# Reading the activations and writing the PSUM banks in woven blocks of four, in a two-layer transformer step

## The chip, the cores and the metric

The kernel runs on one core of one Trainium2 chip. The metric is device time in microseconds, the median of 3 runs of the program. In the views TensorE is named PE, its weight loads PEld, VectorE DVE, ScalarE ACT, GpSimd POOL and SyncE SP.

## What is computed

One inference step of a backbone of two layers on 128 context tokens and 128 latent tokens, with D_MODEL 2048 and float32 weights. Cut to its products:

```python
h = rms_norm(x, g_attn) * (1 + scale1) + shift1
proj = h @ w_in                                           # 2048 x 3584
...
x = x + gate1 * (concat(y_conv, y_g, y_w) @ w_out)        # 2048 x 2048
h2 = rms_norm(x, g_mlp) * (1 + scale2) + shift2
x = x + gate2 * (square(relu(h2 @ w_mlp1)) @ w_mlp2)      # 2048 x 8192, 8192 x 2048
```

Between the two lines of products stand the conv module and two groups of attention heads. `shift`, `scale` and `gate` come from a product of a conditioning vector with `w_ada` (2048 x 12288 per layer). Every weight serves both sets of tokens, so the kernel treats them as 256 columns.

## The kernel before, in words

**The split.** Each product with `w_in`, `w_out`, `w_mlp1` and `w_mlp2` is made to nearly float32 accuracy out of float32r operands. A weight W is split in `hi` (W rounded, ScalarE, L889) and `lo` (W - hi, VectorE, L1219), an activation X in the same way. The kernel adds hi x X_hi, hi x X_lo and lo x X_hi. The activations lie in `hs` (input of `w_in` and `w_mlp1`) and `act2` (input of `w_out` and `w_mlp2`), both `[128, 16, 512]`: for each of 16 k-tiles 256 hi values, one per token, and behind them 256 lo values, 1 KiB each.

**The matmuls.** The weights are the stationary operand, the activations the moving one, and the outputs are features x tokens. A PSUM bank holds 512 float32 values. For each k and each of two output tiles j, one matmul of 512 columns multiplies `hi` with X_hi and X_lo at once and writes the whole bank `pb[2g+j]` (L643, and L742 in the mixers' stage), and one of 256 columns multiplies `lo` with X_hi and adds into the bank's columns 256 to 511 (L646, L745). Per k the order is hi j=0, hi j=1, lo j=0, lo j=1. Four k make a chunk, four chunks a half (g), two halves a pair; a pair covers 512 output features. `walk` sets the order of pairs: 7 for `w_in`, 4 for `w_out`, then 4 times (4 up, 4 down), per layer. All engines follow the same walk.

**The evacuation.** After a half, a bank holds hi x X_hi in its first 256 columns and the other two terms in its last 256. ScalarE copies the last 256 to `tmp` (`copies`, L981), VectorE adds the first 256 to it (L1355 into `tsum` in `pair`; L1418 into `zc` or `zq` and L1426 into `tsum` in the mixers) and raises `bank_freed`. PE waits for `bank_freed` before it writes the same bank again, that is after the other half. The halves that close a norm use one 256-column sum instead, with three matmuls per k and j (`one_sum` L682, L685; `last_slices` L668, L670), and need no `tmp`; the first two pairs of `w_in` (`open_chunk`, L568, L571) also use matmuls of 256 columns.

**The rest of the order.** SP loads weights, 1 MB per DMA, each behind a wait on `lo_ready`. The buffers of `hi` and `lo` form a ring of four chunks: ACT waits for `half_used` (PE done with a chunk) to fill `hi`, DVE waits for `hi_ready`, PE waits for `lo_ready`. POOL loads `w_ada` for the units of L532, which PE multiplies at set places between chunks, with 32 weight columns and four matmuls of 512 columns side by side. L700 in `column_sums` multiplies a float32 matrix of ones with float32 tiles of 256 columns, for the conv module's layer norm. L1255 (`gains`) works out `amul` with operands whose innermost run is the two sets of tokens.

Of the kernel before, what the change touches and what calls it, by code (L numbers as in the profile page):

```python
# [6 lines left out]
ALU = mybir.AluOpType  # L24
ACT = mybir.ActivationFunctionType
AX = mybir.AxisListType

P = 128
# [23 lines left out]
ACT2_LAYER = MIX_STEPS + KT * CHUNKS  # L52
RES_LAYER = KT * (1 + CHUNKS)
UNROLL_K = 4

# [56 lines left out]
def build(nc, t):  # L114
# [93 lines left out]
    sinT = cst[:, C_SIN:C_SIN + P]  # L208
    sel = cst[:, C_SEL:C_SEL + 8]
    sel_q = cst[:, C_SELQ:C_SELQ + 4]  # L210

    def sem(name):
        return nc.alloc_semaphore(name)
# [185 lines left out]
    with block:  # L399
# [97 lines left out]
        def _(pe):  # L497
# [121 lines left out]
            for l in range(DEPTH):  # L619
                def pair(kind, n, i, c, a, last, l=l):  # L620
                    acts = act2 if kind in ("out", "down") else hs
                    for g in range(2):
                        fresh = g == 0 and kind == "up" and isinstance(i, int) and i == 0 \
                            and isinstance(c, int) and c == 0

                        after(pe, bank_freed, 4 * n + 2 * g - 2 - sums_left_out(l, kind))
                        for h in range(4):
                            pe.wait_ge(lo_ready, 8 * n + 4 * g + h + 1)
                            if kind == "down":
                                pe.wait_ge(act2_ready, hidden_base(l, c) + 4 * (h + 1))  # L630
                            elif kind == "up" and not fresh:
                                pe.wait_ge(hs_ready, (2 * l + 1) * NORM_STEPS + 8 * (h + 1))
                            if closes_norm(kind, i, g) and h == 3:
                                mm = last_slices(g, acts)
                            for k in range(4 if not (closes_norm(kind, i, g) and h == 3) else 0):
                                if fresh:
                                    pe.wait_ge(hs_ready, (2 * l + 1) * NORM_STEPS + 8 * h + 2 * (k + 1))
                                k_ = 4 * h + k
                                if closes_norm(kind, i, g):
                                    mm = one_sum(g, h, k, acts)  # L640
                                    continue
                                for j in range(2):
                                    pe.matmul(pb[2 * g + j][:, :], hi[:, h, k, j * P:(j + 1) * P], acts[:, k_, :],  # L643
                                              start=(k_ == 0), stop=False)
                                for j in range(2):
                                    mm = pe.matmul(pb[2 * g + j][:, TOK:2 * TOK], lo[:, h, k, j * P:(j + 1) * P],  # L646
                                                   acts[:, k_, 0:TOK], start=False, stop=(k_ == KT - 1))
                            mm.then_inc(half_used, 1)
                            if last and 4 * g + h in (2, 4, 6):
                                turn_tiles(2 * g + h // 2 - 1)  # L650
                            if a is not None and kind == "out" and h == 2:
                                for u in range(2):
                                    ada_unit(*vector_of(kind, i, a, c), a, 4 * quarter(kind, i, a) + 2 * g + u)
                            if a is not None and kind == "up" and g == 1 and h == 2:
                                for u in range(2 if follows_norm(kind, i, c) else 0, 4):
                                    ada_unit(*vector_of(kind, i, a, c), a, 4 * quarter(kind, i, a) + u)
                    if a is not None and quarter(kind, i, a) == 3:
                        vl, vm = vector_of(kind, i, a, c)
                        ada_turn(vl * VECTORS + vm)
# [79 lines left out]

                def slice_products(g, x, k, slot, acts, start, stop):  # L740
                    for j in range(2):
                        pe.matmul(pb[2 * g + j][:, :], hi[:, slot, k, j * P:(j + 1) * P], acts[:, 4 * x + k, :],  # L742
                                  start=start, stop=False)
                    for j in range(2):
                        mm = pe.matmul(pb[2 * g + j][:, TOK:2 * TOK], lo[:, slot, k, j * P:(j + 1) * P],  # L745
                                       acts[:, 4 * x + k, 0:TOK], start=False, stop=stop)
                    return mm

                def unit(l, u):
# [133 lines left out]
        def _(act):  # L883
# [59 lines left out]
            for l in range(DEPTH):  # L943
# [34 lines left out]
                def copies(kind, n, g, l=l):  # L978
                    for j in range(2):
                        after(act, bank_freed, 4 * n + 2 * g + j - 1 - sums_left_out(l, kind))  # L980
                        act.activation(tmp[:, j, :], pb[2 * g + j][:, TOK:2 * TOK], ACT.Copy).then_inc(tmp_ready, 1)  # L981

                def residual_square(c, i, g, j, l=l):
                    r = res_tiles(l, c) + 4 * i + 2 * g + j
# [229 lines left out]
        def _(dve):  # L1214
# [115 lines left out]
            for l in range(DEPTH):  # L1330
                def pair(kind, n, i, c, a, last, l=l):
# [4 lines left out]
                    for g in range(2):  # L1336
# [6 lines left out]
                        for j in range(2):  # L1343
                            tile = bass.ds(4 * i + 2 * g + j, 1)
                            done = 4 * n + 2 * g + j + 1
                            bank = pb[2 * g + j][:, 0:TOK]
                            if closes_norm(kind, i, g):
                                if j == 0:
                                    dve.wait_ge(first_closed, 2 * l + (kind == "down") + 1)
                                else:  # L1350
                                    dve.wait_ge(half_used, 8 * n + 8)
                                residual(kind, i, g, j, bank.rearrange("p (m q) -> p m q", m=1))
                                continue
                            dve.wait_ge(tmp_ready, done - sums_left_out(l, kind))
                            dve.tensor_tensor(tsum[:, j, :], bank, tmp[:, j, :], ALU.add).then_inc(bank_freed, 1)  # L1355
                            dve.wait_ge(bank_freed, done - sums_left_out(l, kind))
                            if kind == "up":
                                dve.scalar_tensor_tensor(thid[:, j, :], tsum[:, j, :], 0.0, tsum[:, j, :],  # L1358
                                                         ALU.max, ALU.mult).then_inc(relu2_ready, 1)
                            else:  # L1360
                                residual(kind, i, g, j, tsum[:, j:j + 1, :])
# [38 lines left out]
                def mixers(l):  # L1400
                    n = l * PAIRS_LAYER
                    for step in range(OPEN_STEPS if l == 0 else 0, 8 * (IN + 1)):
                        p, g = step // 8, step // 4 % 2
                        for e in range(2 * HEADS):
                            if step == score_step(e) + 1:
                                maxima(l, e)
                        if l == 0 or step:
                            split_lo(n + p, step % 8 + 3)
                        mix_ops(l, step)
                        if step % 4 == 3 and p < IN:  # L1410
                            z, first = (zc, CONV_TILES[p][g]) if p < 2 else (zq, ZQ_TILES[p][g])
                            if p == 5 and g == 0:
                                dve.wait_ge(turn_ready, 4 * l + 2)
                            elif p >= 5:
                                dve.wait_ge(score_ready, 2 * HEADS * l + (2 if p == 5 else 4 + 2 * g))
                            for j in range(2):
                                dve.wait_ge(tmp_ready, 4 * (n + p) + 2 * g + j + 1 - sums_left_out(l, "in"))
                                dve.tensor_tensor(z[:, first + j, :], pb[2 * g + j][:, 0:TOK], tmp[:, j, :], ALU.add)\  # L1418
                                   .then_inc(bank_freed, 1)
                    n += IN  # L1420
                    dve.memset(ssq[:, :], 0.0).then_inc(ssq_steps, 1)
                    for g in range(2):
                        for j in range(2):
                            done = 4 * n + 2 * g + j + 1
                            dve.wait_ge(tmp_ready, done - sums_left_out(l, "out"))
                            dve.tensor_tensor(tsum[:, j, :], pb[2 * g + j][:, 0:TOK], tmp[:, j, :], ALU.add)\  # L1426
                               .then_inc(bank_freed, 1)
                            dve.wait_ge(bank_freed, done - sums_left_out(l, "out"))
                            residual("out", 0, g, j, tsum[:, j:j + 1, :])
                        for j in range(2):  # L1430
                            square_sum(-1, 0, g, j)
# [275 lines left out]
```

## Time and profile before

| | |
|---|---|
| median of 3 runs | 2276.07 us (2275.89 to 2277.03) |
| span of the profiled execution | 2273.1 us |
| PE busy | 2221.1 us, 98% |
| DVE, ACT busy | 1448.4 us (64%), 1140.3 us (50%) |
| granted clock, mean | 0.991 of 2.4 GHz |
| HBM read | 565.76 MB; read and written 250 GB/s over the span |

The profile gives the profiled execution's span, from its first to its last instruction, and no other time of its own; the median is 3.0 us above that span. The ends of matmuls are modelled, and matmuls overlap in the pipeline: a group's mean duration is longer than the distance from one start to the next, and durations of a stage add up to more than the stage.

### The profile page before, as it was taken

What the parts mean: (1) busy time and instruction counts of PE and PEld (TensorE: products, weight loads), DVE (VectorE), ACT (ScalarE), POOL (GpSimd) and SP (SyncE); (2) the same over time, 40 slices, a digit from 0 to 9 for tenths busy, and PEclk for the clock granted to TensorE, in tenths of its full rate; (3) what the DMA queues carried; (4) which work ended last, traced back from release to release, by engine and by line L of the source; (5) the groups of instructions that cost most, each with busy time, mean ns of one, the idle gap of its engine ahead of it and who ended that gap; (6) DMA issues with size and microseconds to landing.
All of it is one profiled execution on the core that took longest, in us unless ns stands there. A gap on an engine that the chain in (4) does not pass through costs nothing. (4 is left out here: it accounts for less than half of the span.)

```text
span 2273.1 us, 36235 instructions
## 1 busy us (share of the span) xinstructions
PE 2221.1 (98%) x13534; PEld 1828.8 (80%) x13534; DVE 1448.4 (64%) x2481; ACT 1140.3 (50%) x1890; POOL 95.6 (4%) x185
## 2 busy tenths in 40 slices
PE   6899999999999999999999999999999999999998
PEld 3577777778877887887787777887788888888887
DVE  2377765755655665565567876676566666666665
ACT  2255664644544444454456466665445545445444
POOL 1000100000000000000000000000000000000000
PEclk8899999999999999999999999999999999999999
DMA  9998878887588578758756877667756556656653
GB/s 377 406 365 304 298 275 316 310 319 260 185 306 323 186 246 309 259 185 305 276 186 239 309 290 282 225 203 260 255 187 187 186 185 186 188 184 200 190 186 106
DMA packets 398512, 570.70 MB, mean 251 GB/s; under 512 B 10232, under 2 KB 356464, under 8 KB 377648
## 3 DMA queue, kind: packets, MB, share of 16 engines
q1 hardware_dynamic: 372368, 398.77, 53.4%
q0 software_dynamic: 23712, 168.08, 18.6%
q10 hardware_dynamic: 2304, 2.10, 0.3%
q8 instruction: 86, 1.41, 0.2%
q14 instruction: 42, 0.34, 0.0%
HBM read 565.76 MB, written 3.15 MB: 250 GB/s over the span
## 5 line engine op out<-in xcount | busy, mean ns | idle before, releaser
L1219 DVE TENSOR_TENSOR lo<-raw,hi 128x1024 fp32r<-128x1024 f32 x688 | 824.7, 1223 | 428.1 <-ACT hi L889 427.0
L889 ACT ACTIVATE hi<-raw 128x1024 fp32r<-128x1024 f32 x688 | 709.7, 1054 | 449.4 <-PE bank L646 308.1
L643 PE MATMUL bank<-act,hi 128*128 128x512 f32 x2304 | 724.7, 396 | 1.2 <-DVE tsum L1426 1.2
L643 PE MATMUL bank<-hs,hi 128*128 128x512 f32 x2048 | 647.0, 397 | 0.2
L646 PEld LDWEIGHTS bank<-act,lo 128*128 128x128 f32 x2304 | 432.8, 188 | 102.3
L646 PEld LDWEIGHTS bank<-hs,lo 128*128 128x128 f32 x2048 | 384.7, 188 | 91.0
L646 PE MATMUL bank<-act,lo 128*128 128x256 f32 x2304 | 452.6, 278 | 0.0
L646 PE MATMUL bank<-hs,lo 128*128 128x256 f32 x2048 | 402.4, 278 | 0.0
L643 PEld LDWEIGHTS bank<-act,hi 128*128 128x128 f32 x2304 | 350.7, 189 | 5.6 <-issue 3.4
L643 PEld LDWEIGHTS bank<-hs,hi 128*128 128x128 f32 x2048 | 311.5, 189 | 20.8 <-issue 20.2
L981 ACT ACTIVATE tmp<-bank 128x256 f32<-128x256 f32 x328 | 108.0, 381 | 357.9 <-PE bank L646 294.3
L742 PE MATMUL bank<-hs,hi 128*128 128x512 f32 x768 | 247.4, 403 | 1.5 <-DVE lo L1219 1.5
L1355 DVE TENSOR_TENSOR tsum<-bank,tmp 128x256 f32<-128x256 f32 x272 | 114.5, 421 | 198.5 <-ACT tmp L981 198.5
L745 PEld LDWEIGHTS bank<-hs,lo 128*128 128x128 f32 x768 | 144.2, 188 | 34.1
L745 PE MATMUL bank<-hs,lo 128*128 128x256 f32 x768 | 151.4, 278 | 0.0
L987 ACT ACTIVATE thid<-xT 128x256 f32 (+1 forms) x160 | 66.8, 418 | 157.5 <-DVE xT L1389 153.5
L742 PEld LDWEIGHTS bank<-hs,hi 128*128 128x128 f32 x768 | 117.3, 189 | 14.5 <-issue 9.5
L532 PE MATMUL bank<-ada,cT 128*32 128x512 f32 x960 | 119.3, 609 | 3.5 <-DMA ada<-in_w_ada 2.6
L474 POOL DMA_DIRECT2D ada<-in_w_ada x120 | 63.6, 530 | 1391.3 <-PE bank L532 1285.9
L1389 DVE SCALAR_TENSOR_TENSOR xT<-tsum,mods,xT 128x128 f32 (+1 forms) x304 | 93.5, 349 | 34.9 <-DVE tsum L1355 33.6
L1509 DVE SCALAR_TENSOR_TENSOR yconv<-hpad,vecs,yconv 128x256 f32<-128x256 f32 x240 | 100.5, 479 | 0.0
L965 ACT ACTIVATE act<-thid 128x256 fp32r<-128x256 f32 x128 | 53.5, 418 | 69.7 <-DVE thid L1358 69.7
(179 smaller groups left out, 1360.0 us busy)
## 6 DMA issues: line engine op xcount, KB each, us to landing
raw<-in_w_mlp SPq DMA_DIRECT2D x256, 1024.0 KB, 6.2
ada<-in_w_ada POOLq DMA_DIRECT2D x120, 1024.0 KB, 7.5
raw<-in_w_in SPq DMA_DIRECT2D x56, 1024.0 KB, 5.9
ring_q<-in_w_ada POOLq DMA_DIRECT2D x40, 1024.0 KB, 11.5
raw<-in_w_out SPq DMA_DIRECT2D x32, 1024.0 KB, 5.5
pre_a<-in_w_ada SPq DMA_DIRECT2D x32, 512.0 KB, 10.8
pre_q<-in_w_ada SPq DMA_DIRECT2D x16, 512.0 KB, 10.6
ada<-in_w_ada SPq DMA_DIRECT2D x16, 512.0 KB, 10.6
```

What stands on the lines that cost most here:

```text
L532: mm = pe.matmul(ada_ps[32 * q:32 * q + 32, :], cT[:, k, :], unit[:, q * 512:(q + 1) * 512], start=(k == 0), stop=(k == KT - 1))
L643: pe.matmul(pb[2 * g + j][:, :], hi[:, h, k, j * P:(j + 1) * P], acts[:, k_, :], start=(k_ == 0), stop=False)
L646: mm = pe.matmul(pb[2 * g + j][:, TOK:2 * TOK], lo[:, h, k, j * P:(j + 1) * P], acts[:, k_, 0:TOK], start=False, stop=(k_ == KT - 1))
L742: pe.matmul(pb[2 * g + j][:, :], hi[:, slot, k, j * P:(j + 1) * P], acts[:, 4 * x + k, :], start=start, stop=False)
L745: mm = pe.matmul(pb[2 * g + j][:, TOK:2 * TOK], lo[:, slot, k, j * P:(j + 1) * P], acts[:, 4 * x + k, 0:TOK], start=False, stop=stop)
L889: act.activation(hi[:, o % 4, :, :], raw_chunk(n, o, s, sub), ACT.Copy).then_inc(hi_ready, 1)
L981: act.activation(tmp[:, j, :], pb[2 * g + j][:, TOK:2 * TOK], ACT.Copy).then_inc(tmp_ready, 1)
L987: act.activation(thid[:, j:j + 1, :], xT[:, bass.ds(4 * i + 2 * g + j, 1), :], ACT.Square).then_inc(sq_ready, 1)
L1219: dve.tensor_tensor(lo[:, o % 4, :, :], raw_chunk(n, o, s, sub), hi[:, o % 4, :, :].bitcast(f32), ALU.subtract).then_inc(lo_ready, 1)
L1355: dve.tensor_tensor(tsum[:, j, :], bank, tmp[:, j, :], ALU.add).then_inc(bank_freed, 1)
L1389: dve.scalar_tensor_tensor(x, total[:, :, s * P:(s + 1) * P], mods[:, l, bass.ds(gate + 4 * i + 2 * g + j, 1), s], x, ALU.mult, ALU.add).t ...
L1509: dve.scalar_tensor_tensor(y, hpad[:, ch, :, tap:tap + P], vecs[:, l, 1, 4 * tap + ch:4 * tap + ch + 1], y, ALU.mult, ALU.add).then_inc(co ...
```

## The change

It alters access patterns alone: no instruction, wait, buffer or DMA is added, removed or moved, and the layout of `hs` and `act2` stays. The hi matmul reads its 512 moving values in blocks of four: four of X_hi, the four of X_lo of the same tokens, the next four of X_hi, and so on (`woven`), and writes the bank in one run, which so holds the two kinds in alternating blocks of four. The lo matmul reads X_hi in order and adds into every second block of four (`strand(bank, 1)`). The evacuations read the bank's two strands in blocks of four (L981, L1355, L1418, L1426). `one_sum`, `last_slices` and `open_chunk` are as before.

```diff
WEAVE = 4
...
@@ -209,6 +193,20 @@
     sel = cst[:, C_SEL:C_SEL + 8]
     sel_q = cst[:, C_SELQ:C_SELQ + 4]
 
+    def woven(tiles, k):
+
+
+        return tiles[:, k, :].rearrange("p (t b e) -> p b t e", t=2, e=WEAVE)
+
+    def strand(bank, t):
+
+
+        return bank.rearrange("p (b t e) -> p b t e", t=2, e=WEAVE)[:, :, t, :]
+
+    def blocks(ap):
+
+        return ap.rearrange("p (b e) -> p b e", e=WEAVE)
+
     def sem(name):
         return nc.alloc_semaphore(name)
 
@@ -640,11 +638,11 @@
                                     mm = one_sum(g, h, k, acts)
                                     continue
                                 for j in range(2):
-                                    pe.matmul(pb[2 * g + j][:, :], hi[:, h, k, j * P:(j + 1) * P], acts[:, k_, :],
+                                    pe.matmul(pb[2 * g + j][:, :], hi[:, h, k, j * P:(j + 1) * P], woven(acts, k_),
                                               start=(k_ == 0), stop=False)
                                 for j in range(2):
-                                    mm = pe.matmul(pb[2 * g + j][:, TOK:2 * TOK], lo[:, h, k, j * P:(j + 1) * P],
-                                                   acts[:, k_, 0:TOK], start=False, stop=(k_ == KT - 1))
+                                    mm = pe.matmul(strand(pb[2 * g + j][:, :], 1), lo[:, h, k, j * P:(j + 1) * P],
+                                                   blocks(acts[:, k_, 0:TOK]), start=False, stop=(k_ == KT - 1))
                             mm.then_inc(half_used, 1)
                             if last and 4 * g + h in (2, 4, 6):
                                 turn_tiles(2 * g + h // 2 - 1)
@@ -739,11 +737,11 @@
 
                 def slice_products(g, x, k, slot, acts, start, stop):
                     for j in range(2):
-                        pe.matmul(pb[2 * g + j][:, :], hi[:, slot, k, j * P:(j + 1) * P], acts[:, 4 * x + k, :],
+                        pe.matmul(pb[2 * g + j][:, :], hi[:, slot, k, j * P:(j + 1) * P], woven(acts, 4 * x + k),
                                   start=start, stop=False)
                     for j in range(2):
-                        mm = pe.matmul(pb[2 * g + j][:, TOK:2 * TOK], lo[:, slot, k, j * P:(j + 1) * P],
-                                       acts[:, 4 * x + k, 0:TOK], start=False, stop=stop)
+                        mm = pe.matmul(strand(pb[2 * g + j][:, :], 1), lo[:, slot, k, j * P:(j + 1) * P],
+                                       blocks(acts[:, 4 * x + k, 0:TOK]), start=False, stop=stop)
                     return mm
 
                 def unit(l, u):
@@ -978,7 +976,7 @@
                 def copies(kind, n, g, l=l):
                     for j in range(2):
                         after(act, bank_freed, 4 * n + 2 * g + j - 1 - sums_left_out(l, kind))
-                        act.activation(tmp[:, j, :], pb[2 * g + j][:, TOK:2 * TOK], ACT.Copy).then_inc(tmp_ready, 1)
+                        act.activation(blocks(tmp[:, j, :]), strand(pb[2 * g + j][:, :], 1), ACT.Copy).then_inc(tmp_ready, 1)
 
                 def residual_square(c, i, g, j, l=l):
                     r = res_tiles(l, c) + 4 * i + 2 * g + j
@@ -1352,7 +1350,8 @@
                                 residual(kind, i, g, j, bank.rearrange("p (m q) -> p m q", m=1))
                                 continue
                             dve.wait_ge(tmp_ready, done - sums_left_out(l, kind))
-                            dve.tensor_tensor(tsum[:, j, :], bank, tmp[:, j, :], ALU.add).then_inc(bank_freed, 1)
+                            dve.tensor_tensor(blocks(tsum[:, j, :]), strand(pb[2 * g + j][:, :], 0), blocks(tmp[:, j, :]),
+                                              ALU.add).then_inc(bank_freed, 1)
                             dve.wait_ge(bank_freed, done - sums_left_out(l, kind))
                             if kind == "up":
                                 dve.scalar_tensor_tensor(thid[:, j, :], tsum[:, j, :], 0.0, tsum[:, j, :],
@@ -1415,16 +1414,16 @@
                                 dve.wait_ge(score_ready, 2 * HEADS * l + (2 if p == 5 else 4 + 2 * g))
                             for j in range(2):
                                 dve.wait_ge(tmp_ready, 4 * (n + p) + 2 * g + j + 1 - sums_left_out(l, "in"))
-                                dve.tensor_tensor(z[:, first + j, :], pb[2 * g + j][:, 0:TOK], tmp[:, j, :], ALU.add)\
-                                   .then_inc(bank_freed, 1)
+                                dve.tensor_tensor(blocks(z[:, first + j, :]), strand(pb[2 * g + j][:, :], 0),
+                                                  blocks(tmp[:, j, :]), ALU.add).then_inc(bank_freed, 1)
                     n += IN
                     dve.memset(ssq[:, :], 0.0).then_inc(ssq_steps, 1)
                     for g in range(2):
                         for j in range(2):
                             done = 4 * n + 2 * g + j + 1
                             dve.wait_ge(tmp_ready, done - sums_left_out(l, "out"))
-                            dve.tensor_tensor(tsum[:, j, :], pb[2 * g + j][:, 0:TOK], tmp[:, j, :], ALU.add)\
-                               .then_inc(bank_freed, 1)
+                            dve.tensor_tensor(blocks(tsum[:, j, :]), strand(pb[2 * g + j][:, :], 0),
+                                              blocks(tmp[:, j, :]), ALU.add).then_inc(bank_freed, 1)
                             dve.wait_ge(bank_freed, done - sums_left_out(l, "out"))
                             residual("out", 0, g, j, tsum[:, j:j + 1, :])
                         for j in range(2):
```

## Rows read from the trace of the kernel before

**Rows 1.** The page: span, and busy time by engine (us, share, instructions).

```profile
span 2273.1 us, 36235 instructions
...
PE 2221.1 (98%) x13534; PEld 1828.8 (80%) x13534; DVE 1448.4 (64%) x2481; ACT 1140.3 (50%) x1890; POOL 95.6 (4%) x185
```

**Rows 2.** The page: the span in 40 slices, PE busy and granted clock, in tenths.

```profile
PE   6899999999999999999999999999999999999998
...
PEclk8899999999999999999999999999999999999999
```

**Rows 3.** Waits of PE and its weight loads: us in all, times, longest.

```profile
PEld bank L643 <- issue: 23.5, 32, 1.2
...
PEld bank L742 <- DVE lo L1219: 4.2, 5, 0.8
...
  PEld bank L643: 1.4, 1
```

**Rows 4.** Groups by shape: busy us, mean ns, idle before.

```profile
L643 PE MATMUL bank<-act,hi 128*128 128x512 f32 x2304 | 724.7, 396 | 1.2 <-DVE tsum L1426 1.2
...
L643 PE MATMUL bank<-hs,hi 128*128 128x512 f32 x2048 | 647.0, 397 | 0.2
...
L742 PE MATMUL bank<-hs,hi 128*128 128x512 f32 x768 | 247.4, 403 | 1.5 <-DVE lo L1219 1.5
...
L742 PE MATMUL bank<-act,hi 128*128 128x512 f32 x128 | 41.1, 402 | 0.7 <-DVE act L1491 0.7
```

**Rows 5.** 1950 to 2200 us: PE, PEld, DVE, ACT, POOL busy (x); then L643 alone.

```profile
1950.00:2200.00 250.00, 250.00 (x1438) 218.12 (x1437) 164.43 (x247) 124.80 (x180) 0.00 (x0) 1.00 0.59 185
...
1950.00:2200.00 250.00, 225.45 (x718) 109.20 (x719) 1.00 0.59 185
```

**Rows 6.** Chain from 1800 to 1812 us: start, us, what.

```profile
1800.34 0.47 PE bank L643 x2
1800.81 0.23 PE bank L646 x2
1801.04 0.46 PE bank L643 x2
```

**Rows 7.** PE at half clock, 39 to 45 us: start, us, instructions.

```profile
39.00:45.00 6.00, 3.75 (x17) 3.75 (x18) 5.60 (x9) 3.74 (x4) 0.00 (x0) 0.50 1.05 407
...
42.70 1.05 PE L568 MATMUL bank<-hs,hi 128*128 128x256 f32 x4
43.56 0.63 PE L571 MATMUL bank<-hs,lo 128*128 128x256 f32 x2
```

**Rows 8.** PE at 1200 us, L668 and L670 by turns, 256 columns each.

```profile
1199.94 0.40 PE L668 MATMUL bank<-act,hi 128*128 128x256 f32 x2
...
1200.66 0.40 PE L668 MATMUL bank<-act,hi 128*128 128x256 f32 x2
```

**Rows 9.** PE at 1407 us: L700; then its durations, min/median/max ns.

```profile
1407.32 1.02 PE L700 MATMUL bank<-ysq,ones 128*128 128x256 f32 x4
...
L700 PE MATMUL bank<-ysq,ones x16: 377/378/381, 266.9 to 1408.0; 128*128 128x256 f32 x16
```

**Rows 10.** Chain, longest pieces: start, us, what.

```profile
1233.32 1.85 PE bank L532 x16
```

**Rows 11.** Groups by shape on DVE and ACT: busy us, mean ns.

```profile
L1219 DVE TENSOR_TENSOR lo<-raw,hi 128x1024 fp32r<-128x1024 f32 x688 | 824.7, 1223 | 428.1 <-ACT hi L889 427.0
...
L889 ACT ACTIVATE hi<-raw 128x1024 fp32r<-128x1024 f32 x688 | 709.7, 1054 | 449.4 <-PE bank L646 308.1 <-PE bank L745 83.0 <-DMA raw<-in_w_in 49.6
...
L1355 DVE TENSOR_TENSOR tsum<-bank,tmp 128x256 f32<-128x256 f32 x272 | 114.5, 421 | 198.5 <-ACT tmp L981 198.5
...
L981 ACT ACTIVATE tmp<-bank 128x256 f32<-128x256 f32 x328 | 108.0, 381 | 357.9 <-PE bank L646 294.3 <-PE bank L745 63.6
...
L1255 DVE SCALAR_TENSOR_TENSOR amul<-mods,vecs 128x8 f32<-128x8 f32 x4 | 0.7, 168 | 0.1
...
L1255 DVE SCALAR_TENSOR_TENSOR amul<-mods,vecs 128x32 f32<-128x32 f32 x3 | 0.6, 185 | 0.0
```

More of the change, by code:

```diff
@@ L54 @@
 UNROLL_K = 4
+WEAVE = 4
 IN_COLS = ((0, 512), (256, 768), (1792, 1024), (1280, 1536), (2048, 3072), (2304, 2560), (2816, 3328))
```

## The prediction, made before the change was run

> **What bounds the kernel now.** First the shares: PE is busy for 2221.1 us of a span of 2273.1, 98%; DVE has 64% and ACT 50% [rows 1], and from the fifth slice on PE is full in every slice at full granted clock (2.4 GHz) [rows 2]. Then the waits of PE: a wait for a filled lo buffer costs L742 4.2 us in all, and L643 stands 23.5 us at "issue" [rows 3]. So the end is set by how fast TensorE takes matmuls from its own stream. Then the groups by shape: 5248 matmuls with the 512-column hi weights' product (2304 + 2048 at L643, 768 + 128 at L742), and as many lo products of 256 columns, since the code issues two of each per k [rows 4].
>
> A duration of 396 ns is not what one costs, since they overlap. The last full stage has 1438 matmuls in 250 us, 718 of them hi [rows 5]: per k (two hi, two lo) 4 x 250/1438 = 0.695 us. The chain splits that: two hi take 0.46 or 0.47 us, two lo 0.23 (17 pairs of each kind stand in these 12 us, all in this beat) [rows 6]. So **a hi costs about 0.233 us and a lo 0.115**. At 2.4 GHz 512 columns are 0.2133 us and 256 are 0.1067: the hi loses 20 ns, the lo 8. The 2624 quads (5248/2) make 2624 x 0.695 = 1824 us, 80% of the span; all that the change can do is there, and the hi excess is 5248 x 0.020 = 105 us.
>
> **What that excess is.** Four sets of rows. (a) The open chunks at half clock: four 256-column matmuls start 0.86 us apart from the next line's (42.70 to 43.56), 0.215 each; 256 columns at 1.2 GHz are 0.2133, so there is almost no excess [rows 7]. (b) The same width at full clock, where hi's two halves are separate instructions: L668 and L670 issue six from 1199.94 to 1200.66 us, 0.12 each, 13 ns over [rows 8]. So it appears only where values are fetched at the fast rate. (c) L700 multiplies plain f32 sums: four of 256 columns are busy 1.02 us, and one is 0.378, so they start (1.02 - 0.378)/3 = 0.214 us apart; that is two cycles a column, 512 cycles for 256 values, as many as a hi has, with the same 128 weights loaded, and no excess [rows 9]. Whether those values come at half pace or twice over, no row says. (d) The adaLN units, four streams side by side: 16 matmuls in 1.85 us, 0.463 for each four, against 0.427 for 1024 cycles: 36 ns over [rows 10]. And the pairs of hi go 0.47, 0.46, 0.47 by turns although nothing but operand addresses differs from k to k [rows 6]. I read this as fetching that collides, over addresses, with the weight fetch or with itself: not DVE, ACT or DMA, which would not keep such a beat.
>
> **The change, part by part.**
> 1. *The hi product's read* (5248 times). It steps 16 bytes in the hi half, 16 bytes in the lo half 1 KiB further on, and so on: 128 blocks. Instruction count, columns and weights are the same. No row of before reads a moving operand in blocks, so I bound it. Best: each half is walked at half pace and the excess goes, as in (c): 0.214 us, a gain of 5248 x 0.019 = 100 us. Worst: one lost cycle of 2.4 GHz at each of 127 block ends, 53 ns: 278 us slower (a halved rate would be 0.427, 1018 us slower). Between them: nothing changes. I take half of the excess recovered, 0.2235 for 0.233: the middle between rows 6 and rows 9, since the pace in each half is that of (c), but the total fetched per cycle is that of the hi now. That is 5248 x 0.0095 = **50 us gained**.
> 2. *The hi product's write*: one run of 512 as before. 0.
> 3. *The lo product* (5248 times) reads one run of 256 and writes 64 blocks of four with gaps of four. No row shows such a write. Lower bound 0 (its start is also tied to the next weight load: below nothing is excluded, as its read is untouched). Upper: a lost cycle at 63 block ends, 26 ns, 138 us in all. I take 0, since the excess above depends on fetching, not on writing: in (c), writes run without loss too.
> 4. *The evacuations.* ACT L981 (328 times, 381 ns) and DVE L1355, L1418, L1426 (328, some 420 ns) now read the bank in blocks of four [rows 11]. DVE has rows with blocks of two: L1255 takes 168 ns for 8 elements and 185 for 32, 0.7 ns an element, while contiguous rows take (1223 - 421)/768 = 1.04: short blocks cost it nothing visible. ACT has none; bound: one element time (L981 against L889 on 1024: (1054 - 381)/768 = 0.88 ns) at each of 63 ends, 55 ns, 18 us of ACT time. Cover: a bank just closed is needed by PE only after the other half's sixteen k, 16 x 0.695 = 11.1 us, and ACT's two copies and DVE's two adds are through in under 2. That cover is missing once, between the w_out pairs: L643 waits 1.4 us for L1426 [rows 3]; four instructions of 55 to 65 ns more give +0.2 us. What queues behind them (the splits of L889 and L1219) has a ring of four buffers, and both engines idle 36% and more.
> 5. *What a faster PE meets.* Everything else keeps its work while quads shrink by 2.7%: DVE in the last stage is at 164.4 of 250 us [rows 5], so it goes to 68%. Weight loads by SP wait on lo_ready, so they come earlier too. A small loss at the adaLN loads: +1 us.
>
> Sum: 2273.1 - 50 + 0.2 + 1 = 2224 in the profile's span. The median of the runs is 2276.07, 3.0 us over the span; I add 3: **2227 us**.
>
> **Rivals.**
> *No change* (0.22). The loss sits in fetching every value at one per cycle whatever its address, or in the weight fetch alone. For it: (d), where more streams give more loss, and the hi at 0.455 ns a column not far from a half at 0.469 (0.120/256). The alternation of 0.47 and 0.46 speaks against a cause without addresses. Time 2276, with evacuations 2274 to 2280. By the Trainium skill (SBUF — State Buffer, The DMA port swizzle) SBUF has lines of 16 bytes, and a read that makes at least two hits in each line has full speed. Blocks of four f32 use each line whole, so by that rule the read costs neither more nor less; no row here shows it.
>
> *The write in blocks stalls TensorE* (0.15): slower. Its place is the lo product, its price up to 26 ns at each of 5248: 2276 + 138 = 2414; it decides as soon as it is over 9.5 ns, where it eats the gain taken above. For it: nothing in the trace writes a bank with gaps. Against: it would have to hit a lo whose fetch already leaves 8 ns open. The Trainium skill (PSUM — Partial Sum Buffer, Specifications (TRN2)) says that any non-contiguous pattern slows matmuls significantly, on account of 8-byte lines; it gives no figure. Blocks of four f32 fill such lines, so the reason given there would spare this write though the rule does not.
>
> *The read in blocks stalls* (0.11): 53 ns at each hi: 2276 + 278 = 2554, 3294 if the rate halves. Against: nothing but the absence of rows.
>
> *A small loss* (0.05): collisions become those of the worse beat everywhere, hi 0.236 and lo 0.120 (rows 6, 8): 5248 x (0.003 + 0.005) = +42, 2318.
>
> **How the numbers follow.** Faster has 0.47: the excess goes with addresses (the beat, L700), and the change alters just these. Its own range is 2176 (all of it gone) to 2268 (a tenth or so). The 8-in-10 range has to take in no change and the write rival: 2176 to 2415; left out are the stalled read (0.11) and bits at both ends. This kernel's measurement tells 0.2% (4.6 us) from nothing: faster by more 0.47, within 0.22, slower 0.31.
>
> **What would show it.** In the last full stage (1950 to 2200 us) the count of matmuls in 250 us: 1438 now, about 1478 by the forecast, 1520 if all the excess goes, 1438 if nothing happens, under 1340 by the write rival. In the chain, two hi under 0.45 us with two lo at 0.23; the write rival shows 0.28 for two lo and 0.47 for hi, the read rival 0.57 for two hi. L981 and L1355 stay at 381 and 421 ns, or show what a block costs; either way PE must not wait for them. The forecast is wrong if the hi pair is still 0.46 to 0.47, or longer; and point 4 is wrong if PE's waits name L1355 or L981.

## The result, and the profile after

The changed kernel takes 2398.13 us (median of 4) against 2276.55: ratio 1.0519, 95% interval 1.0503 to 1.0536, **122 us slower**. The 2276.55 is the median of four runs of the kernel before, the 2276.07 above that of the first three of them. The profiled run has a span of 2396.1 us. Its page (span, busy time):

```profile
span 2396.1 us, 36235 instructions
...
PE 2346.9 (98%) x13534; PEld 1855.6 (77%) x13534; DVE 1454.0 (61%) x2481; ACT 1159.4 (48%) x1890; POOL 95.2 (4%) x185
```

The same instructions, PE as full as before [rows 1], DVE and ACT busy for 6 and 19 us more. The groups by shape (busy us, mean ns, idle before), to be set against [rows 4, 11]; the line numbers have moved, L643 is L641, L646 is L644, L889 is L887, L981 is L979, L1355 is L1353:

```profile
L641 PE MATMUL bank<-act,hi 128*128 128x512 f32 x2304 | 769.8, 416 | 1.0 <-DVE tsum L1425 1.0
L887 ACT ACTIVATE hi<-raw 128x1024 fp32r<-128x1024 f32 x688 | 725.5, 1076 | 527.0 <-PE bank L644 374.8 <-PE bank L743 95.7 <-DMA raw<-in_w_in 48.5
L641 PE MATMUL bank<-hs,hi 128*128 128x512 f32 x2048 | 688.2, 418 | 0.1
...
L979 ACT ACTIVATE tmp<-bank 128x256 f32<-128x256 f32 x328 | 108.6, 383 | 387.9 <-PE bank L644 319.1 <-PE bank L743 68.7
...
L1353 DVE TENSOR_TENSOR tsum<-bank,tmp 128x256 f32<-128x256 f32 x272 | 114.6, 421 | 224.3 <-ACT tmp L979 224.3
```

The hi matmul is 20 ns longer. The evacuations, 381 and 421 ns before, are the same: 383 and 421. ScalarE's split of the weights, which the change does not touch, takes 1076 ns in place of 1054, and that is 16 of ACT's 19 us; PE's waits for the split weights did not grow with it (L740 for L1217: 2.5 us in all, 4.2 before [rows 3]). PE waits no more than it did [rows 3]:

```profile
PEld bank L641 <- issue: 24.2, 31, 1.7
...
PEld bank L641 <- DVE tsum L1425: 1.3, 1, 1.3
```

The window of the last full stage (busy time of PE, PEld, DVE, ACT, POOL with counts) and the chain in it (start, us, what), against [rows 5, 6]:

```profile
1950.00:2200.00 250.00, 250.00 (x1341) 207.09 (x1341) 154.74 (x237) 118.68 (x168) 0.00 (x0) 1.00 0.56 176
```

```profile
1900.21 0.50 PE bank L641 x2
1900.71 0.24 PE bank L644 x2
1900.95 0.51 PE bank L641 x2
```

A quad takes 4 x 250/1341 = 0.746 us in place of 0.695. Two hi went from 0.46 or 0.47 us to 0.50 or 0.51, two lo from 0.23 to 0.24. The difference of 0.051 us times 2624 quads is 134 us, so the matmul stream holds the whole loss, and 11 us more than the 123 by which the spans differ; where those 11 go was not traced. Three things could do it: the hi's read, the lo's write, or both.

### The profile page after: what moved, and what is told of

The parts are those of the page before. It is cut to its first block and busy times, and to the rows that moved or that the text cites. A ratio compares the mean times of both kernels' runs of the same rounds, so it can differ in the third digit from the quotient of the medians.

```text
span 2396.1 us, 36235 instructions
## 1 busy us (share of the span) xinstructions
PE 2346.9 (98%) x13534; PEld 1855.6 (77%) x13534; DVE 1454.0 (61%) x2481; ACT 1159.4 (48%) x1890; POOL 95.2 (4%) x185
## 5 line engine op out<-in xcount | busy, mean ns | idle before, releaser
L1217 DVE TENSOR_TENSOR lo<-raw,hi 128x1024 fp32r<-128x1024 f32 x688 | 829.1, 1224 | 508.3 <-ACT hi L887 504.9
L887 ACT ACTIVATE hi<-raw 128x1024 fp32r<-128x1024 f32 x688 | 725.5, 1076 | 527.0 <-PE bank L644 374.8
L641 PE MATMUL bank<-act,hi 128*128 128x512 f32 x2304 | 769.8, 416 | 1.0 <-DVE tsum L1425 1.0
L641 PE MATMUL bank<-hs,hi 128*128 128x512 f32 x2048 | 688.2, 418 | 0.1
L644 PEld LDWEIGHTS bank<-act,lo 128*128 128x128 f32 x2304 | 434.4, 189 | 146.2
L644 PEld LDWEIGHTS bank<-hs,lo 128*128 128x128 f32 x2048 | 386.4, 189 | 131.1
L644 PE MATMUL bank<-act,lo 128*128 128x256 f32 x2304 | 466.3, 284 | 0.0
L644 PE MATMUL bank<-hs,lo 128*128 128x256 f32 x2048 | 415.2, 285 | 0.0
L641 PEld LDWEIGHTS bank<-act,hi 128*128 128x128 f32 x2304 | 356.5, 190 | 5.4 <-issue 4.2
L641 PEld LDWEIGHTS bank<-hs,hi 128*128 128x128 f32 x2048 | 317.0, 190 | 20.7 <-issue 20.0
L979 ACT ACTIVATE tmp<-bank 128x256 f32<-128x256 f32 x328 | 108.6, 383 | 387.9 <-PE bank L644 319.1
L740 PE MATMUL bank<-hs,hi 128*128 128x512 f32 x768 | 261.3, 422 | 1.4 <-DVE lo L1217 1.4
L1353 DVE TENSOR_TENSOR tsum<-bank,tmp 128x256 f32<-128x256 f32 x272 | 114.6, 421 | 224.3 <-ACT tmp L979 224.3
L743 PE MATMUL bank<-hs,lo 128*128 128x256 f32 x768 | 155.1, 284 | 0.0
L740 PEld LDWEIGHTS bank<-hs,hi 128*128 128x128 f32 x768 | 118.8, 190 | 14.2 <-issue 11.4
```

The source lines that it names most:

```text
L644: mm = pe.matmul(strand(pb[2 * g + j][:, :], 1), lo[:, h, k, j * P:(j + 1) * P], blocks(acts[:, k_, 0:TOK]), start=False, stop=(k_ == KT - 1))
L743: mm = pe.matmul(strand(pb[2 * g + j][:, :], 1), lo[:, slot, k, j * P:(j + 1) * P], blocks(acts[:, 4 * x + k, 0:TOK]), start=False, stop=stop)
L887: act.activation(hi[:, o % 4, :, :], raw_chunk(n, o, s, sub), ACT.Copy).then_inc(hi_ready, 1)
L979: act.activation(blocks(tmp[:, j, :]), strand(pb[2 * g + j][:, :], 1), ACT.Copy).then_inc(tmp_ready, 1)
L1217: dve.tensor_tensor(lo[:, o % 4, :, :], raw_chunk(n, o, s, sub), hi[:, o % 4, :, :].bitcast(f32), ALU.subtract).then_inc(lo_ready, 1)
L1353: dve.tensor_tensor(blocks(tsum[:, j, :]), strand(pb[2 * g + j][:, :], 0), blocks(tmp[:, j, :]), ALU.add).then_inc(bank_freed, 1)
```

## The experiments

All are medians against runs of the kernel before on the same chip (2275.9 to 2278.0 us); brackets are 95% intervals of the ratio.

**1. Read alone, write alone.** In the kernel before, one access is changed (the edit is shown shortened; L742 and L745 have the same), first:

```diff
-    pe.matmul(pb[2 * g + j][:, :], hi[...], acts[:, k_, :], ...)
+    pe.matmul(pb[2 * g + j][:, :], hi[...], woven(acts, k_), ...)
```

> The kernel before, with only the hi product's read in blocks of four; the lo product writes one run of 256 and the banks are evacuated in two runs as before, so the values that meet in a bank are not those of one token and the output is not the reference's. In the changed kernel a quad of matmuls (two hi, two lo) takes 49 ns longer than before: 38 ns on the two hi, 11 on the two lo. Theory R (the read in blocks costs, the write does not): the whole 49 ns, ratio to before 1.05. Theory R+W (each costs where it stands): hi pair 0.505 us as in the changed kernel, lo pair 0.23 as before, so 2276 + 2624 x 0.038 = 2376 us. Theory W (the write in blocks costs, and the hi pair only shows it): hi pair 0.467 us and 2276 us, nothing lost.

and, apart from it:

```diff
-    mm = pe.matmul(pb[2 * g + j][:, TOK:2 * TOK], lo[...], acts[:, k_, 0:TOK], ...)
+    mm = pe.matmul(strand(pb[2 * g + j][:, :], 1), lo[...], blocks(acts[:, k_, 0:TOK]), ...)
```

> The kernel before, with only the lo product's write in every second block of four; the hi product reads and writes one run of 512 and the banks are evacuated in two runs, so the sums land on other tokens' values and the output is not the reference's. Theory R: 2276 us, hi pair 0.467 and lo pair 0.231 as before. Theory R+W: lo pair 0.242, hi pair unchanged, 2276 + 2624 x 0.011 = 2305 us. Theory W: all the loss, 2398 us.

The read alone: 2396.84 us, 1.0530 [1.0512, 1.0547]. The write alone: 2276.51 us, 1.0002 [0.9992, 1.0012]. The chain of the one, and of the other:

```profile
1900.42 0.50 PE bank L658 x2
1900.92 0.24 PE bank L661 x2
```

```profile
1899.86 0.47 PE bank L658 x2
1900.33 0.23 PE bank L661 x2
```

The read makes all of the loss (theory R). It even makes the lo pair's 0.24: there the lo product reads and writes one run, as before, and is yet slower, so a part of what the hi's read loses shows only in the starts behind it. ScalarE's split takes 1077 ns in the kernel with the read alone and 1054 in the one with the write alone, so it is TensorE's read that lengthens it too.

**2. The size of a block.** `WEAVE = 4` becomes 16, 2 and 64; the computation stays.

> The changed kernel with blocks of sixteen (64 bytes) in place of four, everything else and the computation the same. Theory B (each end of a block costs the same): 31 ends in a hi in place of 127, so the 19 ns of a hi become 4.6 and the 5.6 of a lo 1.3; 2276 + 5248 x 0.006 = 2307 us. Theory C (the two read places 1 KiB apart collide with each other or with the weight load, whatever the length of a block): the loss stays within a third of the changed kernel's 122 us, 2360 to 2400. Theory L (a line longer than 16 bytes is fetched and used in part): the loss goes altogether once a block fills the line, 2276 us.

> The changed kernel with blocks of two (8 bytes), everything else and the computation the same. Theory B: 255 ends in a hi and 127 gaps in a lo, twice the cost: 2276 + 2 x 122 = 2520 us. Theory C: about the changed kernel's 2398. A fetch unit of 16 bytes that is used in half: a hi needs 256 fetches for 128, far more than twice the loss; a hi would go to 0.4 us or over and the time to some 3200 us.

> The changed kernel with blocks of 64 (256 bytes), the computation the same. Blocks of 2, 4 and 16 cost 522, 121 and 42 us. There are 7 block ends in a hi. Theory B' (a price per block end, some 0.25 to 0.3 ns at 1 KiB apart as blocks of sixteen show): 2276 + 5248 x 7 x 0.28 ns = 2286 us. Theory C' (while both places move on together, each hi has a fixed loss besides): over 2295 us.

| bytes in a block | block ends in a hi | us | over before | ratio |
|---|---|---|---|---|
| 8 | 255 | 2798.09 | 522 | 1.2296 [1.2276, 1.2317] |
| 16 (the change) | 127 | 2398.13 | 122 | 1.0519 [1.0503, 1.0536] |
| 64 | 31 | 2317.72 | 42 | 1.0177 [1.0160, 1.0194] |
| 256 | 7 | 2276.56 | 0 | 0.9997 [0.9987, 1.0007] |

Over 5248 hi the losses are 99, 23, 8 and 0 ns for each, so 0.39, 0.18, 0.26 and 0 ns for each block end: no one price per end fits. None of the theories gave these numbers. B missed with blocks of sixteen values (42 us, not 31) and of two (522, not 244), and B' with blocks of 64 (0, not 10). C missed with sixteen and two, C' with 64, and L with sixteen, where the loss did not go. The half-used unit of 16 bytes wanted some 3200 us with blocks of two, and it was 2798. The lo's write and the evacuations change with `WEAVE` too and were not tried apart at these sizes. But with blocks of two the chain has the loss in the hi, 0.66 us for two, and two lo still take 0.24; the copies and adds take 382 and 422 ns:

```profile
1900.37 0.66 PE bank L641 x2
```

**3. The distance between the two places.** In the changed kernel the step from the hi place to the lo place is set to another number of elements (256 in the change), so other values are read, in the same number, blocks and order:

```diff
-        return tiles[:, k, :].rearrange("p (t b e) -> p b t e", t=2, e=WEAVE)
+        view = tiles[:, k, :].rearrange("p (t b e) -> p b t e", t=2, e=WEAVE)
+        dims = list(view.ap)
+        dims[2] = (252, dims[2][1])
+        return bass.AP(view.tensor, view.offset, dims)
```

> The changed kernel, but the second read place of the hi product lies 252 elements (1008 bytes, one block less) behind the first in place of 256 (1 KiB); it reads values that belong four tokens before, so the output is not the reference's, with the same number of columns, blocks and writes. Reading alone costs the loss, as the read-only kernel has shown (2396.8 us with the write in one run). Theory D (the loss comes from two read places exactly 1 KiB apart, which meet in the same part of SBUF): the hi pair comes most of the way back from 0.505 to 0.467 us, 2276 to 2320 us. Theory H (leaving a run costs at every block, wherever the next one lies): 2398 us and a hi pair of 0.505.

> As the kernel with 252 elements, but 240 (960 bytes, 64 less than 1 KiB): it tells whether the distance that matters is one block or a larger step. Theory D: 2276 to 2320 us here at least, if it was not so at 1008 bytes. Theory H: 2398 us.

> As that kernel with 224 elements (896 bytes, 128 less than 1 KiB). If the loss falls steadily as the distance leaves 1 KiB, it lies under the 59 us of 960 bytes; if the period is 64 bytes with a phase inside it, it equals the 59 us (960 and 896 are both multiples of 64) and 1008 is the odd one.

> As that kernel with 160 elements (640 bytes, 128 over 512). A period of 256 or 512 bytes that is symmetric gives what 896 bytes (128 under 1024) gave, 2333 us; if only the direction behind a multiple of 512 costs, 2276 us or less.

> As that kernel with 192 elements (768 bytes). If parts of SBUF repeat every 256 bytes, 768 meets as 512 and 1024 do: 2398 us. If they repeat every 512 bytes, 768 is the furthest point of the period: 2335 us or less.

> As that kernel with 128 elements (512 bytes) between the two places, again wrong values. Theory P (parts of SBUF repeat with a period that divides 512 bytes, so 512 meets as 1024 does): 2398 us. Theory F (the further apart the worse, or only 1 KiB meets): between 2276 and 2335 us.

> The changed kernel with 132 elements (528 bytes) between the two read places, wrong values again. 16 bytes apart it ran 72 us faster than before, 512 and 1024 bytes apart 121 slower. Theory P (only the distance within 512 bytes counts: 528 is 16): 2205 us. Theory S (16 bytes gains because each line is read twice in a row): over 2276 us, and near the 2351 of 1008 bytes, which lies one line on the other side of a multiple of 512.

> The changed kernel with the second read place only one block (16 bytes) behind the first, so the hi product reads blocks 0, 1, 1, 2, 2, 3, ...: the same three-level pattern with 128 blocks, but no far jump. It reads wrong values for the lo half, so the output is not the reference's. So far 1 KiB apart costs 122 us over before, 1008 bytes 75, 960 bytes 59. Theory N (a part of the loss is the price of the nested pattern itself, whatever it points at, the rest is the distance): at least some 50 us stay, 2325 us. Theory D (all of it lies in where the two places are): 2276 us or less.

| bytes apart | over a multiple of 256 | us | over before | ratio |
|---|---|---|---|---|
| 1024 (the change) | 0 | 2398.13 | 122 | 1.0519 [1.0503, 1.0536] |
| 768 | 0 | 2395.64 | 120 | 1.0528 [1.0510, 1.0545] |
| 512 | 0 | 2397.65 | 121 | 1.0518 [1.0491, 1.0545] |
| 528 | 16 | 2398.67 | 123 | 1.0536 [1.0519, 1.0554] |
| 640 | 128 | 2335.53 | 60 | 1.0256 [1.0239, 1.0273] |
| 896 | 128 | 2333.16 | 56 | 1.0247 [1.0230, 1.0264] |
| 960 | 192 | 2335.30 | 59 | 1.0266 [1.0249, 1.0283] |
| 1008 | 240 | 2351.32 | 75 | 1.0328 [1.0311, 1.0345] |
| 16 | 16 | 2205.17 | -72 | 0.9689 [0.9672, 0.9705] |

Half of the loss is a matter of address: distances of 512, 768 and 1024 bytes lose twice what 640, 896 and 960 lose. Something repeats every 256 bytes; a period of 128 is ruled out by 640 and 896, one of 64 by these and 960. The other half, some 57 us, is there at every far distance tried. So at 1008 and 960 bytes theory D (2320 us at most) and theory H (2398) both missed. At 16 bytes, where the order is block 0, 1, 1, 2, 2, 3, the kernel runs faster than the one before: N missed and D came true there alone. The same remainder in 528 bytes loses 123, so that gain is no matter of phase: P missed with its 2205 us, and of S only the sign came true, not the nearness to 1008.

One reading fits 528 and 1008; no run was made for it. What may count is not the distance within a pair alone but how far apart in the order of reads two blocks stand whose addresses differ by a multiple of 256. At 512, 768 and 1024 bytes a block of X_hi and the second block right behind it differ by such a multiple. At 528 the second block and the next one of X_hi do (528 - 16 = 512), again neighbours in the order, and the loss is the same. At 1008 it is a block of X_hi and the second block of the next pair (1008 + 16 = 1024), three reads on, and the loss is 75 us. At 640, 896 and 960 no two blocks so near do.

**4. What the gain at 16 bytes is.** Distance 0 (each block of X_hi twice in a row), and the whole run of 256 values twice, `dims = [dims[0], (0, 2), (1, TOK)]`:

> The changed kernel with both read places the same: the hi product reads each block of X_hi twice in a row and no X_lo, so the lo terms of the activations are left out. With 16 bytes apart a hi costs 0.216 us. If that comes from lines read again at once, a hi costs 0.214 to 0.217 here too and the time is 2205 us; if it came from the distance 16, distance 0 meets as 256 does and it is 2398.

> The same values left out, but X_hi is read in one run of 256 and then the same run again: as many different lines as above, each read again only after 63 others. If the gain needs the line at once, the hi is as before, 0.233 us, and the time 2276; if it needs only fewer different lines in a matmul, 2205.

Distance 0: 2206.82 us, 0.9697 [0.9681, 0.9713]. The same run twice: 2276.10 us, 0.9997 [0.9988, 1.0007]. The chains:

```profile
1900.01 0.43 PE bank L644 x2
1900.44 0.23 PE bank L647 x2
```

```profile
1899.94 0.47 PE bank L644 x2
1900.40 0.23 PE bank L647 x2
```

Both came as "at once" wants. Both read the same values, 64 different blocks of 16 bytes, each of them twice; only the order differs. Read again at once, a hi takes 0.215 us, two ns over 512 cycles of 2.4 GHz; read again after 63 others it takes 0.233, and so does every hi of the kernel before. So nearly all of the excess of 20 ns belongs to the moving fetch: it comes when each block of 16 bytes differs from the one before it. What in the fetch sets it, these runs do not show.

**5. The weight loads.** Two kernels leave out three quarters of the hi product's weight columns from the second k on, so most features lack their sum; the first is built on the kernel before, the second on the changed one. The third moves the weight tiles by 128 bytes:

```diff
+    w = P if k_ == 0 else 32
-    pe.matmul(pb[2 * g + j][:, :], hi[:, h, k, j * P:(j + 1) * P], ...)
+    pe.matmul(pb[2 * g + j][0:w, :], hi[:, h, k, j * P:j * P + w], ...)
```

```diff
     raw = place("raw", [P, 4, 8, 256], f32)
+    craw = place("craw", [P, S, KT], f32)
     hi = place("hi", [P, 4, 4, 256], f32r)
```

> The kernel before, but the hi product uses only 32 of its 128 weight columns from the second k on, so only the first 32 features of each tile get their full sum; the moving operand, its 512 columns and all waits are the same. Per quad 320 weight columns are fetched in place of 512. Theory W (the excess of 57 ns a quad over 640 comes from weight fetches that collide with the moving operand's): it falls to about 57 x 320/512 = 36 ns, 2276 - 2624 x 0.021 = 2221 us, and the two lo gaps differ least from before in the hi's own weight loads. Theory S (the moving fetch alone is too slow for one f32 value per cycle): 2276 us, hi pair 0.467.

> The changed kernel with the same 32 weight columns in the hi product. Theory W for the loss by blocks: it is smaller than with full weights, 122 x 320/512 = 76 us over the narrow kernel of before. Theory S or H: the same 122 us over it.

> The kernel before, with a small tile placed ahead of the hi weights, so that hi and lo weights lie 128 bytes further on against the activations; computation and instructions the same. Theory W (weight fetch and moving fetch meet by their addresses; it is what makes two hi take 0.463 and 0.469 us by turns): the beat changes and the time moves by more than 4 us, either way. Theory own (the moving fetch's excess is its own): 2276 us and the same gaps.

Narrow before: 2269.47 us, 0.9972 [0.9962, 0.9981]: 7 us gained of the 55 that theory W wanted. And these are not gained in the steady stream: its last full stage has 1439 matmuls in 250 us, against 1438 before [rows 5]. What is shorter is the first pair of hi after an adaLN unit of L532, 0.57 us here and 0.67 before:

```profile
1950.00:2200.00 250.00, 250.00 (x1439) 189.55 (x1439) 164.55 (x251) 123.13 (x181) 0.00 (x0) 1.00 0.60 189
```

```profile
1228.36 1.85 PE bank L532 x16
1230.22 0.57 PE bank L744 x2
```

```profile
1235.17 0.67 PE bank L742 x2
```

With 80 units (1280 matmuls of L532, 16 in each) some 0.1 us at each would make 8 us, an estimate that covers the 7. Narrow after: 2395.61 us, 126 over it, where W wanted 76. Weights moved: 2278.02 us, 1.0007 [0.9997, 1.0017], within 0.2% of none; but the beat has changed, two hi now take 0.46 at every turn and two lo 0.24 or 0.23:

```profile
1901.33 0.46 PE bank L643 x2
1901.79 0.24 PE bank L646 x2
1902.03 0.46 PE bank L643 x2
```

So the weights' address does shift single starts by a few ns, and the sum stays. Neither fewer weight columns in the hi (a quarter of them) nor other weight addresses changed the excess in the steady stream, and the loss by the woven read did not shrink with the weights either.

## Why the prediction was wrong

It forecast 2227 us and faster with 0.47. The measured 2398 lies in the stated range, on the other side of no change; the range reached that far for the sake of the write rival, which was not the cause. The prediction's own sign of being wrong, a hi pair of 0.46 to 0.47 or longer, came: 0.50 to 0.51.

**What bounds the kernel** held: the matmul stream takes the change and nothing else answers to it. So did the quad of 0.695 us, and the split in hi and lo.

**The reading of the excess is where it failed** ("What that excess is"). The prediction took four observations and concluded that fetches collide over addresses. (a) and (b), that the excess comes with the fast rate, agree with the runs. The beat of 0.47 and 0.46, which "speaks against a cause without addresses", was real but small: moving the weights altered it and gained nothing. And (c), L700, was read as a sign that walking each half at half pace removes the excess. The runs show otherwise: it goes when the same 16 bytes are asked for twice in a row (0.215 us), and does not go for the same lines later on. L700 gives one value two cycles; that it profits in the same way is likely, but was only argued. The text said itself that no row told how those values come.

**Step 1** then took half of a gain for which no row spoke, against a price of 53 ns for block ends as the other bound. Measured is a loss of 23 ns for each hi, 19 or so in the hi's own starts (0.505/2 against 0.233) and the rest in the starts of the lo behind it. The middle between two bounds on either side of zero was a number without a mechanism.

**Step 2 and step 3** (the writes cost 0) held: the write alone gave 1.0002 [0.9992, 1.0012] for the lo's, and the hi's stayed one run. The rival of the write in blocks, with 0.15 and 2414 us, is nearest to the measured time and wrong in its cause. Its count of matmuls in the last stage (under 1340) all but came too, with 1341; the chain told the two apart, with 0.24 for two lo where it wanted 0.28. By the Trainium skill (PSUM — Partial Sum Buffer, Specifications (TRN2)) any non-contiguous pattern slows matmuls significantly; this write of 16-byte blocks with 16-byte gaps does not, so here the measurement decides against the rule as it is worded.

**The rival of the read in blocks** (0.11, 2554 us) had the right place, the hi's read; its price of one lost cycle at each end was mis-sized: 278 us forecast, 122 measured, and not a price per end at all. It got the smallest chance but one, with the note that nothing spoke against it but the absence of rows.

**The rival of no change** saw a fetch that is slow whatever the address. For one run of values that is what section 4 shows, but for the woven read the address counts (section 3). By the Trainium skill (SBUF — State Buffer, The DMA port swizzle) two hits in a line are enough for full speed. The runs disagree: four hits in each line lost 122 us at 1 KiB apart, and a hi that reads one run, also with four hits in each line, takes 0.233 us where the block read twice in a row gives 0.215. The same passage of the Trainium skill adds that each access that crosses to a new line costs. The 0.233 against 0.215 agrees with that; the 122 us do not follow from it, since the woven read crosses as often as the one run does.

**Step 4** held: L979 383 ns, L1353 421 ns, L641 waits 1.3 us for L1425 (1.4 before). **Step 5** had nothing to meet, since PE became slower; DVE's share in the last stage fell from 66% to 62% (154.74 of 250).

What stays open: why far places lose 57 us even away from multiples of 256 bytes, whether the order of reads is what makes 528 and 1008 bytes apart so unlike, and what makes blocks of 8 bytes cost over four times those of 16.

No read pattern over the same 512 values was found that beats the kernel before. The two patterns that do (2205 and 2207 us) read about half of the values only; blocks of 256 bytes equal it.

## What to carry to other kernels

A float32r matmul whose moving operand is one run of 512 values already pays some 9% over its columns at 2.4 GHz for the fetch, so its access pattern is no free choice: keep runs of 256 bytes (64 bytes already lost 42 us here), and where two places must be read by turns in shorter blocks, keep their distance off multiples of 256 bytes and off the blocks right beside such a multiple (528 bytes lost as much as 512, and 1008 more than 960). In this kernel the pattern of the lo's write and of the evacuation was free to follow, down to blocks of four values. And where a bound spans gain and loss and no row lies between, forecast no change or measure one instruction with the new pattern first.

## What the runs showed of the hardware

- The moving fetch goes by whether a block is the one just read: a 16-byte block read twice in a row lets 512 float32r columns pass in 0.215 us (2205 us for the kernel), different blocks take 0.233, and blocks alternating 1 KiB apart 0.25.
- Two read places by turns lose 120 to 122 us when they lie 512, 768 or 1024 bytes apart and 56 to 60 when 640, 896 or 960; one block beside a multiple of 256 it is 123 us (528) and 75 (1008).
- Blocks of 8 bytes cost 522 us, two hi 0.66 us; blocks of 256 bytes cost nothing (0.9997).
- TensorE's read pattern lengthens ScalarE's split of 1024 values: 1054 ns before, 1077 with the woven read alone, 1054 with the write alone, and 1052 at 1008 bytes apart.
- Loading only a quarter of the hi's weight columns leaves the steady stream as it is (1439 against 1438 matmuls in 250 us) and shortens the first pair of hi after an adaLN unit from 0.67 to 0.57 us.
- Writing a bank in 16-byte blocks with 16-byte gaps, accumulating, costs TensorE nothing (1.0002), and neither ScalarE nor VectorE reads them slower (383 and 421 ns).
